# A decoder layer in one kernel: attention steps for two heads regrouped, gate-weight splits moved forward, and two waits of the last feed-forward tile changed

## The reference

```python
h = modulate(rms_norm(x, g_ffn1[i]), sh1, sc1)
x = x + 0.5 * (1.0 + gt1[:, None, :]) * swiglu(h, w1_ffn1[i], w3_ffn1[i], w2_ffn1[i])
h = modulate(rms_norm(x, g_mix[i]), sh2, sc2)
cq, ckv, kidx, widx, mq, mk, mv, ga, gb = split_cols(h @ w_in[i])
y_dsa = dsa_attention(cq, ckv, kidx, widx, ...) @ w_proj_dsa[i]      # top 128 keys of a query, 8 heads of 64
y_moba = moba_attention(mq, mk, mv) @ w_proj_moba[i]                 # causal, 8 heads of 64
y = jax.nn.sigmoid(ga) * y_dsa + jax.nn.sigmoid(gb) * y_moba
x = x + (1.0 + gt2[:, None, :]) * (y @ w_out[i])
h = modulate(rms_norm(x, g_ffn2[i]), sh3, sc3)
x = x + 0.5 * (1.0 + gt3[:, None, :]) * swiglu(h, w1_ffn2[i], w3_ffn2[i], w2_ffn2[i])
return rms_norm(x, g_final)
```

## Time and profile before

| | us |
|---|---|
| median of three runs | 1172.1 |
| lowest and highest | 1171.39, 1172.57 |
| the profiled execution | 1171.75 |
| its span, first to last instruction | 1169.9 |
| TensorE busy with matmuls | 1141.6 |
| VectorE busy | 543.0 |
| ScalarE busy | 486.2 |
| attention loop, 534.8 to about 696.6 | 162 |

### The profile page before, as it was taken

The page is one execution under the profiler, slowest core; times in us unless marked ns, Lnnn a source line. Parts: engine busy times, 40 slices in busy tenths (PEclk is TensorE's granted clock), DMA queues, the critical chain, the costliest instruction groups (busy, mean ns, idle before and its releaser), DMA issues.

```text
span 1169.9 us, 14947 instructions
## 1 busy us (share of the span) xinstructions
PE 1141.6 (98%) x5529; PEld 912.2 (78%) x5529; DVE 543.0 (46%) x892; ACT 486.2 (42%) x860; POOL 158.7 (14%) x98
## 2 busy tenths in 40 slices
PE   5999999999999999999999999999999999999997
PEld 4688888888888878676777778887888888888887
DVE  3534454444344354479786546545333333332231
ACT  4555655556444232134555555334223232232223
POOL 0135444454333210000000000000000000000000
PEclk9999999999999999999999999999999999999999
DMA  9845645655555342222222113322242242243211
GB/s 310 267 144 186 225 163 179 212 183 172 169 170 170 90 116 74 54 55 73 55 55 55 54 56 90 90 73 72 72 126 89 72 135 80 77 143 99 85 63 73
DMA packets 159099, 138.25 MB, mean 118 GB/s; under 512 B 3551, under 2 KB 157522, under 8 KB 159058
## 3 DMA queue, kind: packets, MB, share of 16 engines
q1 hardware_dynamic: 130948, 109.38, 30.0%
q10 hardware_dynamic: 28110, 28.32, 7.4%
HBM read 135.59 MB, written 2.10 MB: 118 GB/s over the span
## 4 chain that ended last, share of the span: by engine, by line
PE 90%; DVE 6%; ACT 1%; issue 0%; POOLq 0%; POOL 0%; DVEq 0%; ACTq 0%
PE ps L352 26%; PE ps L354 26%; PE ps L353 26%; PE ps L1057 2%; PE ps L1032 2%; PE ps L1042 2%; DVE score L1377 1%; PE ps L383 1%; DVE max L1375 1%; DVE w_lo L331 1%; PE ps L980 1%; DVE h_lo L439 1%; PE ps L887 1%; DVE nrm L433 1%; PE ps L481 1%; DVE score L1365 0%
## 5 line engine op out<-in xcount | busy, mean ns | idle before, releaser
L331 DVE TENSOR_TENSOR w_lo<-raw,w_hi 128x1024 fp32r<-128x1024 f32 (+1 forms) x164 | 239.3, 1460 | 419.5 <-ACT w_hi L326 419.5
L352 PE MATMUL ps<-h_hi,w_hi 128*128 128x512 f32 x1024 | 407.4, 398 | 5.3 <-DVE h_lo L439 5.0
L354 PE MATMUL ps<-h_hi,w_lo 128*128 128x512 f32 x1024 | 399.9, 390 | 0.0
L353 PE MATMUL ps<-h_lo,w_hi 128*128 128x512 f32 x1024 | 399.6, 390 | 0.0
L326 ACT ACTIVATE w_hi<-raw 128x1024 fp32r<-128x1024 f32 (+1 forms) x164 | 183.2, 1118 | 266.5 <-PE ps L354 266.2
L352 PEld LDWEIGHTS ps<-h_hi,w_hi 128*128 128x128 f32 x1024 | 192.8, 188 | 53.6 <-issue 8.0
L354 PEld LDWEIGHTS ps<-h_hi,w_lo 128*128 128x128 f32 x1024 | 192.6, 188 | 40.9
L353 PEld LDWEIGHTS ps<-h_lo,w_hi 128*128 128x128 f32 x1024 | 192.9, 188 | 37.9 <-issue 0.5
L352 PE MATMUL ps<-g_hi,w_hi 128*128 128x512 f32 x330 | 129.8, 393 | 0.2 <-DVE w_lo L331 0.2
L354 PE MATMUL ps<-g_hi,w_lo 128*128 128x512 f32 x330 | 128.6, 390 | 0.0
L353 PE MATMUL ps<-g_lo,w_hi 128*128 128x512 f32 x330 | 128.5, 389 | 0.0
(11 more groups left out here) (182 smaller groups left out, 939.0 us busy)
## 6 DMA issues: line engine op xcount, KB each, us to landing
raw<-in_w_ffn SPq DMA_DIRECT2D x42, 1024.0 KB, 5.4
ada<-in_w_ada ACTq DMA_DIRECT2D x27, 1024.0 KB, 5.1
raw<-in_w_ffn SPq DMA_DIRECT2D x16, 1408.0 KB, 6.3
raw<-in_w_in SPq DMA_DIRECT2D x64, 256.0 KB, 3.2
ada<-in_w_ada SPq DMA_DIRECT2D x16, 512.0 KB, 8.8
raw<-in_w_out SPq DMA_DIRECT2D x16, 256.0 KB, 3.1
x_tok<-in_x SPq DMA_DIRECT2D x4, 512.0 KB, 5.1
raw<-in_w_ffn SPq DMA_DIRECT2D x8, 256.0 KB, 7.6
```

What stands on the lines that cost most here:

```text
L331: nc.vector.tensor_tensor(tiles_of(w_lo[j % SPL], nk), raw_of(f, j, nk), tiles_of(w_hi[j % SPL], nk).bitcast(F32), ALU.subtract).then_inc( ...
L352: nc.tensor.matmul(ps[:, bank, :], hi, rhs_hi, start=start, stop=False)
L353: nc.tensor.matmul(ps[:, bank, :], hi, rhs_lo, start=False, stop=False)
L354: return nc.tensor.matmul(ps[:, bank, :], lo, rhs_hi, start=False, stop=stop)
```

## The change

Three edits. (1) The attention loop treats a pair in three steps instead of four: the chunks of 128 and 256 keys share a step, in which a head's two score blocks lie side by side in one bank (columns 0 to 127 and 128 to 383). Such a step has bias, exponentials and scaling per head and chunk, but one block of transposes and one copy per head. There are 24 steps with five gate tiles each, and one or two selections per step of VectorE. In each step of ScalarE the split of a gate unit now comes first, in VectorE's it follows the bias, ahead of the selections. (2) In the last tile's two halves TensorE waits for the residual of the tile that had the half's own bank, not for both before the first half. (3) In the down projections ScalarE splits the second weight unit of the next tile ahead of the square, except after the last tile.

```diff
             u, h = U_DOWN[1] + 2 * (KD - 1), SEQ // 2
-            pe.wait_ge(x_done, KD * 4 - 1)
             for part in range(2):
+                pe.wait_ge(x_done, KD * 4 - 2 + part)
                 for q in range(2):
...
+                if d < KD - 1:
+                    hi_u(act, U_DOWN[f] + 2 * d + 3)
                 act_square(act, 1 + 2 * f, d)
                 if f:
                     act_final(act, d)
-                hi_u(act, U_DOWN[f] + 2 * d + 3)
+                if d == KD - 1:
+                    hi_u(act, U_DOWN[f] + 2 * d + 3)
...
-        steps = [(b, hp, c) for b in range(2) for hp in range(HP) for c in range(QT)]
+        CHUNKS = (((0, 0), (1, P)), ((2, 0),), ((3, 0),))
+        SPP = len(CHUNKS)
+        steps = [(b, hp, cs) for b in range(2) for hp in range(HP) for cs in CHUNKS]
...
-            take = min(4, GATE_TILES - given)
+            take = min(5, GATE_TILES - given)
...
             def scores(m):
+                for n, (c, at_) in enumerate(cs):
+                    for e in range(2):
+                        o = 64 * e
+                        last = nc.tensor.matmul(ps[:, B_S[e], at_:at_ + (c + 1) * P], q[o:o + 64, hp, c * P:(c + 1) * P],
+                                                k[o:o + 64, hp, 0:(c + 1) * P], start=True, stop=True)
+                        if n == len(cs) - 1:
+                            last.then_inc(s_psum, 1)
...
             for m in range(NST + 3):
+                for g in gates_ended(m - 1):
+                    hi_u(act, U_GATE + g + 2)
                 if m < NST:
                     exps(m)
-                if m >= 6 and (m - 6) % QT == 0:
-                    o_high((m - 6) // QT)
+                if m >= SPP + 2 and (m - SPP - 2) % SPP == 0:
+                    o_high((m - SPP - 2) // SPP)
                 if 1 <= m < NST + 1:
                     copies(m - 1)
                 for g in gates_ended(m - 1):
-                    hi_u(act, U_GATE + g + 2)
                     nc.scalar.activation(gate[g][:, :], ps[:, 4 + g % 2, :], ACT.Copy).then_inc(evac, 1)
...
-                if selected < 2 * TOPK // 8:
+                for g in gates_ended(m - 1):
+                    lo_u(dve, U_GATE + g + 2)
+                for _ in range(min(1 + m % 2, 2 * TOPK // 8 - selected)):
                     select(selected)
                     selected += 1
                 if m < NST:
                     normalise(m)
-                if m >= 6 and (m - 6) % QT == 0:
-                    o_low((m - 6) // QT)
-                for g in gates_ended(m - 1):
-                    lo_u(dve, U_GATE + g + 2)
+                if m >= SPP + 2 and (m - SPP - 2) % SPP == 0:
+                    o_low((m - SPP - 2) // SPP)
```

More of the change, by code:

```diff
@@ L778, in dve_mods, with keys_of @@
             dve.wait_ge(mod_done, 7)
-        steps = [(b, hp, c) for b in range(2) for hp in range(HP) for c in range(QT)]
+        CHUNKS = (((0, 0), (1, P)), ((2, 0),), ((3, 0),))
+        SPP = len(CHUNKS)
+        steps = [(b, hp, cs) for b in range(2) for hp in range(HP) for cs in CHUNKS]
         NST = len(steps)
+        def keys_of(m):
+            return sum((c + 1) * P for c, _ in steps[m][2])
         B_S, B_T, B_O = (0, 1), (2, 3), (6, 7)
@@ L1029, in scores @@
                 pe.wait_ge(m_done, 2 * m)
-                for e in range(2):
-                    o = 64 * e
-                    nc.tensor.matmul(ps[:, B_S[e], 0:(c + 1) * P], q[o:o + 64, hp, c * P:(c + 1) * P],
-                                     k[o:o + 64, hp, 0:(c + 1) * P], start=True, stop=True).then_inc(s_psum, 1)
+                for n, (c, at_) in enumerate(cs):
[5 more added lines that the diff above has]
+                            last.then_inc(s_psum, 1)
             def transposes(m):
-                c = steps[m][2]
                 for e in range(2):
@@ L1040, in transposes @@
                         pe.wait_ge(pt_done, 2 * m + e - 1)
-                    for s in range(c + 1):
+                    for s in range(keys_of(m) // P):
                         last = nc.tensor.transpose(ps[:, B_T[e], s * P:(s + 1) * P], prob[m % 2][:, e, s * P:(s + 1) * P],
@@ L1046, in values @@
             def values(m):
-                b, hp, c = steps[m]
+                b, hp, cs = steps[m]
                 v = (mv, dv)[b]
@@ L1052, in values @@
                     pe.wait_ge(vt_done, QT)
-                if pair >= 2 and c == 0:
+                if pair >= 2 and m % SPP == 0:
                     pe.wait_ge(olo_done, pair - 1)
-                for s in range(c + 1):
-                    for e in range(2):
-                        last = nc.tensor.matmul(ps[64 * e:64 * e + 64, B_O[pair % 2], c * P:(c + 1) * P],
-                                                v[:, s, hp * P + 64 * e:hp * P + 64 * e + 64], probT[:, e, s * P:(s + 1) * P],
-                                                start=s == 0, stop=s == c)
+                for c, at_ in cs:
+                    for s in range(c + 1):
+                        for e in range(2):
+                            last = nc.tensor.matmul(ps[64 * e:64 * e + 64, B_O[pair % 2], c * P:(c + 1) * P],
+                                                    v[:, s, hp * P + 64 * e:hp * P + 64 * e + 64],
+                                                    probT[:, e, at_ + s * P:at_ + (s + 1) * P], start=s == 0, stop=s == c)
                 last.then_inc(pv_done, 1)
@@ L1197, in exps @@
             def exps(m):
-                c = steps[m][2]
+                cs = steps[m][2]
                 for e in range(2):
-                    i = 2 * (m % 2) + e
-                    p = prob[m % 2][:, e, 0:(c + 1) * P]
                     act.wait_ge(m_done, 2 * m + e + 1)
-                    nc.scalar.activation(p, p, ACT.Exp, bias=nmax[:, i, :], scale=-1.0,
-                                         accum_out=psumq[:, i, :]).then_inc(e_done, 1)
+                    for n, (c, at_) in enumerate(cs):
+                        i = 4 * (m % 2) + 2 * e + n
+                        p = prob[m % 2][:, e, at_:at_ + (c + 1) * P]
+                        last = nc.scalar.activation(p, p, ACT.Exp, bias=nmax[:, i, :], scale=-1.0, accum_out=psumq[:, i, :])
+                    last.then_inc(e_done, 1)
             def copies(m):
-                c = steps[m][2]
+                w = keys_of(m)
                 if m:
@@ L1401, in biased @@
             def biased(m):
-                b, hp, c = steps[m]
-                w = (c + 1) * P
-                d = score[:, c - 1, 0:w] if b and c else dist[:, SEQ - w:SEQ]
+                b, hp, cs = steps[m]
                 if m >= 2:
```

35 lines of the change are left out of this document (21 added, 14 removed).

## The result

The changed kernel takes 1165.42 us (median of four runs, 1165.0 to 1165.88), the kernel before 1172.29 beside it (four runs, 1171.39 to 1172.57): 0.9945 of the time, interval 0.9931 to 0.9959, or 6.9 us less. The forecast was 5.2 less, 1166.9, with a range of 1165.3 to 1169.4. The profiled executions took 1171.75 and 1165.01, 6.74 apart, with spans of 1169.87 and 1163.28.

The account below looks back on a forecast made before the run. TensorE was taken as the bound, busy 1141.6 of 1169.9 us, with slack at block edges. Terms summed to -3.6 us in the loop and -1.6 in the last tile, 1172.1 - 5.2 = 1166.9 us; range 1165.3 to 1169.4.

Parts of the forecast that it names:

- Step 1: Attention loop, gate blocks: 32 blocks become 26, each edge costing 0.20 us; 1.2 us less.
- Step 6: Loop's middle, branch change: the values' 0.60 us wait goes, 0.6 less; the split for gate tile 8, late next, costs nothing.
- Step 7: Loop's end: the last values' 0.80 us wait goes, 0.8 less; the merge waits for o_lo, 0.3 more.
- Step 3: Attention loop, transposes: 0.11 us each and no cost per block; eight blocks less give 0.2 us more.
- Step 4: Attention loop, score blocks: nothing gained, the 0.2 us besides the keys put on the records; 1.6 us kept for the range.
- Step 5: Loop's start: 0.6 us less wait for ScalarE's copy of the values, 0.3 us more for the first probabilities.
- Step 9: Last output tile: waits for the other bank's residual, 1.0 us, and the second weights, 0.63, both go; 1.6 us less.
- 2 value blocks: Attention loop, value blocks: 0.15 us a block besides the records; eight blocks less, 1.2 us less.
- the edges stay: Rival, attention loop: TensorE's lost time belongs to the matmuls, terms 1 to 3 fall away; 1169.1 us, chance 0.13.
- the last tile gains nothing: Rival, last output tile: some other wait, its g rows or its weights, ends at the same time; 1168.5 us, chance 0.05.
- scores gain too: Rival, attention loop: the 0.2 us of scores belongs to the step, 1.6 us less; 1165.3 us, chance 0.08.
- Step 8: Splits moved ahead of ScalarE's exponentials and VectorE's selections: no cost, what queues behind is wanted a step later; nothing.

Follow-up runs that it names:

- last_tile: The kernel before with both last-tile edits (each half waits only for its own bank's residual; split ahead of square), loop as before; 1170.2 us, ratio 0.9986.
- split_scores: The changed kernel with the joint step's scores in two blocks again, 128 keys, then the values, then 256 keys; 1167.77 us, ratio 0.9968.
- copy_first: The changed kernel with ScalarE's copy of a finished gate moved up behind the gate's split, ahead of exponentials and copies; 1165.27 us, ratio 0.9936.
- best: The changed kernel with the gate's copy early, o_hi and o_lo ahead of the splits, two gate tiles ahead of the first value tile; 1164.1 us, ratio 0.9929.
- splits_last: The changed kernel with the gate splits late again, ScalarE's ahead of the gate's copy, VectorE's at the step's end; 1170.39 us, ratio 0.9984.
- one_select: The changed kernel with one VectorE selection a step instead of one or two, five left ahead of the mask in step 12; 1175.46 us, ratio 1.0028.
- mask_early: The kernel before with a second selection in step 12, so that none is left ahead of its mask at step 16; 1172.21 us, one run.
- out_first: The changed kernel with the gate's copy moved up behind its split, and o_hi and o_lo ahead of the gate splits; 1164.77 us, one run.

## Why the prediction was right, and where it was off

The sign, the range and most terms held; the size was 1.7 short of the medians' difference of 6.9, 1.5 short of that between the profiled executions. The time lies 0.1 us inside the range's lower end, which was put there for the one term that came at its other end, the scores. The errors partly cancel: steps 1, 6 and 7 brought 1.2 less than forecast, steps 3, 4, 5 and 9 brought 2.2 more, so that the sum came nearer than its terms. 0.4 of the 1.5 lies ahead of the loop and belongs to no edit. For the rest, all distances between starts in TensorE's timeline of the loop were summed by kind of block, with the idle time taken out (us, number of blocks):

```
         scores        values        transposes    gate tiles    value tiles   idle
before   23.83 (32)    22.31 (32)    17.01 (32)    93.64 (32)    1.94 (2)      3.03
after    22.14 (24)    21.11 (24)    17.01 (24)    92.93 (26)    1.94 (2)      1.72
```

| step | forecast | measured | from |
|---|---|---|---|
| 1 gate blocks | -1.2 | -0.7 | the sums; an edge is 0.20 before and 0.22 after |
| 2 value blocks | -1.2 | -1.2 | the sums |
| 3 transposes | +0.2 | 0.0 | the sums |
| 4 scores | 0 | -1.7 | the sums; 0.85 against 1.06 a joint step |
| 5 start | -0.6 +0.3 | -0.4 +0.0 | idle 0.83 for 1.27; 0.39 for 0.36 |
| 6 middle | -0.6 | -0.6 +0.5 | 0.60 gone, 0.50 new |
| 7 end | -0.8 +0.3 | -0.8 +0.5 | 0.80 gone; the merge's segment 0.54 longer |
| 9 last tile | -1.6 | -1.84 | segments; `last_tile` alone: -1.82 |

The loop's rows make -4.9, its segment's difference, and with the 0.5 of the merge -4.4, where the forecast has -3.6.

*Step 1:* the price of an edge is right, but a late gate's copy inside a gate block makes an edge more: in step 12 the block is broken by a wait, the matmul after it is followed after 0.31 us instead of 0.227, and the block is 0.25 longer without the idle time; in step 20 it is 0.15 longer in the same place. These 0.4 are most of what is missing.

*Step 3* came out at nothing by luck. Blocks of transposes of one size take the same in both kernels (0.63 for six, 0.85 for eight), so eight blocks less cost the forecast 0.2. But in the kernel before, the transposes next to the waits at the start and at the end took 0.34 more than their kind, in the changed kernel 0.13, and that covers it.

*The busy time held slack*, as the prediction read it off against the full busy time of the earlier trace rows; the rival in which the edges stay is excluded by the blocks of the pair, and the one in which the last tile gains nothing by `last_tile`.

*Step 4 is the one that failed.* It said that "short matmuls pay per matmul" and took nothing. It took the price of score blocks from the transposes, a block of another kind. `split_scores` showed the other end: 0.2 us a block. The rival "scores gain too" happened, at the size it had (1.6 there, 1.7 measured). The earlier trace rows already held a hint: 384 keys at 0.85 and 256 at 0.63 leave about 0.2 at no keys, with four records in each; equal numbers of records can't say whether the record or the block pays. The joint step is the first with eight.

*Step 6 was right that the wait goes, wrong that nothing follows.* "What is late next" was taken to be the split for gate tile 8. It was ScalarE's copy of the gate, which stands behind the exponentials and the copies of the step. Timelines of VectorE, ScalarE and TensorE of the changed kernel in step 12, whose scores start at 608.49:

```profile
608.85 1.49 DVE L1410 TENSOR_TENSOR score<-score,dist 128x256 f32<-128x256 f32 x3
...
611.05 0.40 ACT L1216 ACTIVATE prob<-prob,nmax 128x128 f32<-128x128 f32 x1 [2.96 <-DVE nmax L1423]
...
612.82 1.05 ACT L1225 ACTIVATE probT<-ps 128x512 f32<-128x512 f32 x2
613.78 0.58 ACT L1241 ACTIVATE gate<-ps 128x512 f32<-128x512 f32 x1
...
614.50 0.47 PE L352 MATMUL ps<-h_hi,w_hi 128*128 128x512 f32 x1 [0.50 <-ACT gate L1241]
```

The mask and its distances hold VectorE until 610.3, ScalarE waits 2.96 for the bias, and the copy, ready to be made since step 11 ended, comes last. The next gate unit's tiles need its bank. Three edits that the prediction looked at one by one (mask, split ahead, copy behind) meet in one queue. `copy_first` removes it.

*Step 5:* the gain was 0.2 smaller, the new wait 0.3 smaller, and the sign named for it, waits for the first probabilities of 0.5 or more together, did not appear (0.39). `best` showed why the two can't be taken apart: ScalarE's copy ends the first wait, but VectorE's queue ends the second, so what is won in front of the first comes back there.

*Step 7:* the wait for `o_lo` was forecast at 0.3 and is 0.35; a further 0.19 is the restart. A wait costs more than its idle time: in the kernel before, the first half-width matmul after the wait is followed after 0.22 us instead of 0.12. Two such restarts are the 0.2 by which step 9 was too small.

*Step 8* was right that the earlier splits cost nothing, except through `o_lo`. It didn't ask what the step would cost without them: 3.1 us by `splits_last`, loop and merge together (3.5 without its late start), more than half of the loop's gain. With five tiles a step the reordering is a condition of the regrouping, not an addition to it.

*Step 9* added 1.0 and 0.63 as independent terms. Their sum is right, since both edits are made, but the parts aren't: 0 and 0.7 alone.

VectorE as the bound and the falling clock stayed rivals: no transposes wait for scaling after step 1, and the clock of the loop is 1.00. The first of them also counted one step too many: only the odd steps 1 to 9 have two selections, since step 11 finds one left, so it is five steps and 7.5 us, not six and 9. `one_select` showed both, in step 12 alone: with the selections put off until the mask, VectorE holds TensorE, and the clock falls while it stands.

## What to carry to other kernels

Where an engine looks full, compare the distance between starts in a long row of equal instructions with what a block of them takes from its first start to the next block's: the difference times the number of blocks is what regrouping can bring, and it has to be read for each kind of block. Two waits of one engine in a row are not two terms: the second takes over what the first gives back unless its own chain is moved too, so test them alone and together. After moving work to the front of an in-order queue, list what is now last in it and who waits for that, above all in the one step with extra work.

## What the runs showed of the hardware that was not expected

- A block of score matmuls (64 rows, four or eight of them) costs 0.2 us besides its columns, as the gate blocks do (0.20 to 0.22) and the value blocks (0.15), while transposes between two such blocks show none. In the timeline of the weight loads, scores have 0.35 us without a load ahead of them, values 0.12 to 0.76, transposes 0.17 and gate tiles none.
- A wait of TensorE costs more than its idle time: 0.07 us at the change of branch, 0.10 in the last tile, 0.19 at the merge, 0.25 inside the gate block of step 12.
- In `one_select` the granted clock fell while TensorE stood for 7.9 us, and it was 0.50 for the four microseconds after, which cost 1.8 us. A wait of 2.14 in `splits_last` left it at 1.00 (618 to 622). On this the Trainium skill bears ("TensorE: Matmul & The Clock Gate", section "Part 1: The HAM clock gate (the "warmup" mystery)"): an idle engine goes back to half the clock. By that rule, the rows of `one_select` agree.
- Ahead of the loop the clock differs from execution to execution of equal instructions. The stretch from 451 to 455, kernel before, is in the earlier trace rows with 0.57; in the changed kernel and in `best`:

```profile
451.00:455.00 4.00, 4.00 (x15) 3.29 (x16) 1.50 (x10) 0.00 (x0) 0.00 (x0) 0.61 0.50 131
```

```profile
451.00:455.00 4.00, 4.00 (x29) 3.61 (x30) 2.72 (x11) 0.83 (x2) 0.00 (x0) 1.00 0.28 67
```

In the three executions that start their loop late the clock is low a second time. From 504 to 508, in `copy_first`:

```profile
504.00:508.00 4.00, 3.94 (x11) 2.35 (x10) 3.20 (x7) 2.70 (x6) 0.00 (x0) 0.59 0.51 133
```

In `splits_last` and `mask_early` it is 0.57 there, in `last_tile` and `out_first` 1.00. So `last_tile` and `best`, with starts at 534.19 and 534.48, have the clock at 1.00 in both places, the three latest have it low in both, and all others (534.39 to 535.52) in the first alone. No edit touches these places. The spread of 2.4 us in the loop's start is as large as half of the loop's gain, and it is why the segments, not single times, carry the comparisons here. Why the clock stays up in some executions wasn't tried.
